# Shift and scale by output blocks, and R, K and V added up in six banks as inputs and weights arrive

## The chip, the cores and the metric

The kernel runs on one core of a Trainium2 chip. Its time is the device time of one execution in microseconds (us), the median of several. The first phase, which the change touches, is some 320 us of 3357. TensorE (PE) multiplies matrices, VectorE (DVE) and ScalarE (ACT) work on elements, GpSimd (POOL) and SyncE (SP) issue transfers here.

## What is computed

A trunk of two layers. Layer 0 mixes in time with RWKV-7, layer 1 with a pooling mixer; behind each comes a mixture of experts. The part that matters here is the beginning of layer 0, up to the scan:

```python
cond = jax.nn.silu(c)
mod = (cond @ ada_w[i] + ada_b[i]).reshape(B, N_MOD, D_MODEL)[:, :, None, :]
shift1, scale1, gate1, shift2, scale2, gate2 = (mod[:, n] for n in range(N_MOD))
h = x * (1 + scale1) + shift1
...
xx = jnp.pad(h, ((0, 0), (1, 0), (0, 0)))[:, :-1] - h
xs = h[None] + xx[None] * mu[:, None, None, :]
r, k, v = jnp.einsum('nbsd,nde->nbse', xs[:3], w_rkv)
w = -jax.nn.softplus(-(w0 + jnp.tanh(xs[3] @ w1) @ w2).astype(f32)) - 0.5
a = jax.nn.sigmoid(a0 + (xs[4] @ a1) @ a2)
g = jax.nn.sigmoid(xs[5] @ g1) @ g2
kk = (k * k_k).astype(f32).reshape(B, S, H, N)
kk = kk * lax.rsqrt(jnp.maximum(jnp.sum(kk * kk, axis=-1, keepdims=True), 1e-24))
```

There are 512 positions and 1024 columns (D), all float32. `w1` and `a1` have 64 columns, `g1` has 160. The modulation of both layers has 12 vectors of 1024: two of them (the shift and scale of `h`) are needed at once, ten later.

## The kernel before

The program is a row of phases with a barrier of all engines behind each. `phase_rwkv_products` is the first. D is cut in KT = 8 blocks of 128, the positions in TT = 4 tiles of 128; HALF is 512 columns.

**Modulation.** `cond` is one column for each block of 128 inputs. DVE multiplies a row block of `ada` (128 inputs x 1024 columns) by its column and adds it to an accumulator: eight such steps for one vector (lines 271 and 274 for the first two, 306 and 309 for the other ten, `add_mod`). PE then adds up the 128 partitions by products with a column of ones, eight for a vector (L352 for the first two, L361 in `sum_mod` for the others). SP loads the first two vectors' blocks into the buffers of `xs`, POOL the 80 blocks of the others into the four slots of `rw_g`, each when DVE is through with the block before it in that slot.

**Operands.** When both vectors are complete DVE makes `h` block by block (L287) and from it `xs[n]` in two instructions for each block: `shift_part` (L292) and `own_part` (L297). `xs` has two slots of 8 blocks, n goes to slot n % 2, and n >= 2 waits until the product that read the slot is through (`last_use`). The additions of `add_mod` stand in DVE's row behind the operands 1, 2 and 3 (`mods_after`: three vectors, three, four).

**Products.** PE makes one output of 128 x 512 after the other (`product`, L376) in a ring of four PSUM banks: eight matmuls that add up over the blocks of D, then ACT takes the bank (L432). R and K are made transposed, eight outputs of 128 columns each; V in four tiles of positions for each half of the columns. Each matmul of float32 leaves two rows in the trace. K's outputs are also squared (L442) and summed by head on PE (L383). The weights of R, K and V come in halves of 2 MB (SP, L228, L230 and L235) into two buffers, each when the products of the half before it in that buffer are done. `sum_mod` stands ahead of ten of the products (`sums_before`). Then follow the low-rank products: tanh (64 columns), decay `s` (65 rows with the bias), `ta` (64), the rate `aT` (eight outputs), `tg` (128 and 32 columns), the gate `g` (eight tiles of two matmuls).

**End.** PE turns the summed modulation columns (L420), DVE copies them (L344), SP stores them to `mod_rows` in HBM (L244). SP loads the constants of the scan into `held` (L242) when the last product that reads it is done, and waits for both. ACT's evacuations of the gate wait until the 80 additions are through, since they write `rw_g`. The next phase, the scan, begins on DVE at L632.

## Time and profile before

| | |
|---|---|
| median of 3 executions | 3357.09 us (3357.06 to 3357.4) |
| the profiled execution | 3357.63 us, span 3355.8 |
| mean granted clock of TensorE in it | 0.984 |
| PE busy | 3203.0 us, 95% of the span |
| DVE busy | 2593.2 us, 77% |
| first phase, up to the next one's first DVE instruction | 320.9 us |

Times of the trace count from the start of the span. A timeline names the start, the time from the first to the last instruction of a merged row, engine, line, output and inputs, shapes and count, and behind it in brackets how long the engine had been idle and what released it. The granted clock (PEclk) is 1.00 at 2.4 GHz and 0.5 at 1.2 GHz.

### The profile page before, as it was taken

What the parts mean: (1) busy time and instruction counts of PE and PEld (TensorE: products, weight loads), DVE (VectorE), ACT (ScalarE), POOL (GpSimd) and SP (SyncE); (2) the same over time, 40 slices, a digit from 0 to 9 for tenths busy, and PEclk for the clock granted to TensorE, in tenths of its full rate; (3) what the DMA queues carried; (4) which work ended last, traced back from release to release, by engine and by line L of the source; (5) the groups of instructions that cost most, each with busy time, mean ns of one, the idle gap of its engine ahead of it and who ended that gap; (6) DMA issues with size and microseconds to landing.
All of it is one profiled execution on the core that took longest, in us unless ns stands there. A gap on an engine that the chain in (4) does not pass through costs nothing. (4 is left out here: it accounts for less than half of the span.)

```text
span 3355.8 us, 56990 instructions
## 1 busy us (share of the span) xinstructions
PE 3203.0 (95%) x21428; PEld 2750.4 (82%) x21428; DVE 2593.2 (77%) x4747; ACT 1164.2 (35%) x1787; POOL 2053.4 (61%) x1303
## 2 busy tenths in 40 slices
PE   4998999799999999999999988999999999999998
PEld 2443888689999999888888866999999998888886
DVE  6672665479998888499888764899988866988997
ACT  0112455233324443333333432333344433333333
POOL 0211444267776555788888712677765558888884
PEclk9998999899999999999999989999999999999999
DMA  7870001267777887999999822687778979999995
GB/s 272 291 246 27 3 4 54 74 242 261 268 241 253 317 301 275 383 344 346 351 357 347 290 82 79 237 274 269 257 238 317 327 273 382 350 344 361 348 345 180
DMA packets 366859, 856.31 MB, mean 255 GB/s; under 512 B 32681, under 2 KB 201105, under 8 KB 358322
## 3 DMA queue, kind: packets, MB, share of 16 engines
q1 hardware_dynamic: 281394, 542.98, 46.8%
q0 software_dynamic: 85248, 310.42, 25.9%
q8 instruction: 139, 2.28, 0.3%
q14 instruction: 78, 0.64, 0.1%
HBM read 750.46 MB, written 102.81 MB: 254 GB/s over the span
## 5 line engine op out<-in xcount | busy, mean ns | idle before, releaser
L1683 PE MATMUL peer_acc<-peer_hhi,peer_uhi 128*128 128x384 f32 x2048 | 696.8, 340 | 8.9 <-POOL peer1same_ulo L1883 4.5
L1683 PE MATMUL peer_acc<-peer_hlo,peer_uhi 128*128 128x384 f32 x2048 | 685.8, 335 | 0.0
L1883 POOL TENSOR_TENSOR peer0same_ulo<-peer_u,peer_uhi 128x1024 fp32r<-128x1024 f32 x128 | 311.9, 2438 | 193.5 <-ACT peer_uhi L1763 192.8
L1883 POOL TENSOR_TENSOR peer1same_ulo<-peer_u,peer_uhi 128x1024 fp32r<-128x1024 f32 x128 | 312.0, 2439 | 191.8 <-ACT peer_uhi L1763 190.4
L1683 PEld LDWEIGHTS peer_acc<-peer_hhi,peer_uhi 128*128 128x128 f32 x2048 | 386.0, 188 | 12.5 <-POOL peer1same_ulo L1883 5.8
L1759 ACT ACTIVATE peer_gel<-peer_acc 128x384 f32<-128x384 f32 x256 | 125.9, 492 | 752.3 <-PE peer_acc L1683 677.6
L1683 PEld LDWEIGHTS peer_acc<-peer_hlo,peer_uhi 128*128 128x128 f32 x2048 | 385.9, 188 | 1.0 <-issue 0.5
L1914 POOL TENSOR_TENSOR peer0lsame_vlo<-peer0l_v,peer0l_vhi 128x1024 fp32r<-128x1024 f32 x128 | 310.8, 2428 | 85.2 <-ACT peer0l_vhi L1798 84.4
L1914 POOL TENSOR_TENSOR peer1lsame_vlo<-peer1l_v,peer1l_vhi 128x1024 fp32r<-128x1024 f32 x128 | 309.5, 2419 | 86.4 <-ACT peer1l_vhi L1798 85.3
L1946 DVE SCALAR_TENSOR_TENSOR peer_acc<-peer_row,peer_p_g,peer_acc 128x1024 f32<-128x1024 f32 x254 | 325.2, 1280 | 36.7 <-DMA peer_row<-in_pe_v,peer_idx 34.5
L1683 PE MATMUL peer_acc<-peer_hhi,peer0same_ulo 128*128 128x384 f32 x1024 | 343.6, 336 | 0.0
L1683 PE MATMUL peer_acc<-peer_hhi,peer1same_ulo 128*128 128x384 f32 x1024 | 343.4, 335 | 0.0
L1936 DVE SCALAR_TENSOR_TENSOR peer_row<-peer_row,peer_acc 128x1024 f32<-128x1024 f32 x256 | 308.4, 1206 | 0.1
L1722 PE MATMUL peer_acc<-peer0l_vhi,peer0l_phi 128*128 128x512 f32 x768 | 299.7, 390 | 3.7 <-DVE peer0l_plo L2044 2.3
L1722 PE MATMUL peer_acc<-peer1l_vhi,peer1l_phi 128*128 128x512 f32 x768 | 299.0, 389 | 2.8 <-DVE peer1l_plo L2044 1.5
L1722 PE MATMUL peer_acc<-peer0lsame_vlo,peer0l_phi 128*128 128x512 f32 x768 | 299.3, 390 | 0.0
L1722 PE MATMUL peer_acc<-peer0l_vhi,peer0l_plo 128*128 128x512 f32 x768 | 299.2, 390 | 0.0
L1722 PE MATMUL peer_acc<-peer1l_vhi,peer1l_plo 128*128 128x512 f32 x768 | 298.8, 389 | 0.0
L1722 PE MATMUL peer_acc<-peer1lsame_vlo,peer1l_phi 128*128 128x512 f32 x768 | 298.8, 389 | 0.0
L1864 POOL DMA_INDIRECT peer_row<-in_pe_v,peer_idx x256 | 271.5, 1061 | 42.5 <-issue 15.0
L1864 POOL DMA_INDIRECT peer_row<-in_pe_u,peer_idx x256 | 256.7, 1003 | 64.2 <-issue 38.9
L1763 ACT ACTIVATE peer_uhi<-peer_u 128x1024 fp32r<-128x1024 f32 x250 | 262.9, 1052 | 19.8 <-DMA peer_u<-in_pe_uT 19.8
(431 smaller groups left out, 6890.6 us busy)
## 6 DMA issues: line engine op xcount, KB each, us to landing
peer_u<-in_pe_uT SPq DMA_DIRECT2D x256, 512.0 KB
peer0l_v<-in_pe_v SPq DMA_DIRECT2D x128, 512.0 KB
peer1l_v<-in_pe_v SPq DMA_DIRECT2D x128, 512.0 KB
activations<-peer_gel SPq DMA_DIRECT2D x256, 192.0 KB
rw_g<-in_ada POOLq DMA_DIRECT2D x80, 512.0 KB
routing<-peer0m_wb SPq DMA_DIRECT2D x24, 1024.0 KB, 8.4
peer0l_wt<-routing SPq DMA_DIRECT2D x64, 384.0 KB
peer0l_gl<-activations SPq DMA_DIRECT2D x128, 192.0 KB
```

The lines of the kernel that those rows point to most:

```text
L1683: mm = pe.matmul(ub[e % 2][:, 0:SD], a, h[:, k, 0:SD], start=(n == 0), stop=(n == 3 * KT - 1))
L1722: mm = pe.matmul(acc[:, t, ds], a[:, ts], w[:, ds], start=(begin and n == 0), stop=(end and n == 2), skip_group_check=True)
L1759: a.activation(gel[:, e % NL], ub[e % 2][:, 0:SD], ACT.Gelu).then_inc(gel_made, 1)
L1763: a.activation(uhi[:, n % NH], u[:, n % NU], ACT.Copy).then_inc(uhi_made, 1)
L1864: g.indirect_dma_start(row[:, at % NG], None, table, bass.IndirectOffsetOnAxis(ap=idx[:, s:s + 1], axis=0)).then_inc(row_loaded[at % NG], 16)
L1883: g.tensor_tensor(ulo[:, q].rearrange("p k e -> p (k e)"), u[:, q].rearrange("p k e -> p (k e)"), uhi[:, e % NH].bitcast(F32).rearrange("p ...
L1914: g.tensor_tensor(vlo[:, q], vr[:, q], vhi[:, e % NH].bitcast(F32), ALU.subtract).then_inc(vlo_made, 1)
L1936: v.scalar_tensor_tensor(out=row[:, s % NG], in0=row[:, s % NG], scalar=1.0, in1=h_g, op0=ALU.mult, op1=ALU.mult, accum_out=dots[:, s:s + ...
L1946: v.scalar_tensor_tensor(out=acc_g, in0=row[:, s % NG], scalar=p_g[:, s:s + 1], in1=acc_g, op0=ALU.mult, op1=ALU.add).then_inc(acc_made, 1)
```

## The change

The host lays the first two modulation vectors out by blocks of output columns. A load now holds all 1024 inputs for 128 columns of one vector. For each block `k` of 128 columns:

- DVE adds up both vectors for these columns (`sum_first`, one tensor_scalar and seven scalar_tensor_tensor of 256 elements, each waiting for the one before). PE sums the partitions (two products with ones), DVE copies two columns and adds the bias, and makes `h` and `xs[0]` of this block. In DVE's row `sum_first(k + 1)` stands ahead of `make_h(k)`.
- PE takes the block as soon as it is there (`step`): six outputs in six PSUM banks get one matmul each. After eight steps the six are complete, and the two that are left are made as before (`rest`). K and V go the same way.
- The weights come in blocks of 128 rows x 1024 columns (0.5 MB) into twelve slots, eight of their own and four of `rw_s`. SP issues R's in turn with modulation and input blocks.

The ring has six banks instead of four. The first blocks' buffers are `rw_kT` and `rw_aT`. The tanh product stands behind V's steps and ahead of its two rests. `xs[5]` is made ahead of `xs[4]`, and the gate's first products ahead of the rate's. Four gate tiles stand ahead of the rate's eight outputs and four behind. The transpose of the modulation columns stands last. The ten vectors are added behind the operands 1, 2, 3 and 4 (two, four, two, two), and the reciprocal of the norm stands behind all of them.

```diff
-        w = arena("w", [P, 2, KT, HALF])
+        OWN, MORE = KT, TT
+        w_own = arena("w", [P, OWN, D])
+        w = [w_own[:, n] for n in range(OWN)] + [rw["s"][:, n] for n in range(MORE)]
...
+        NF = 4
+        first_w = [rw[n][:].rearrange("p k s -> p (k s)")[:, 2 * D * b:2 * D * b + 2 * D].rearrange("p (m k q) -> p m k q", m=2, q=P)
+                   for n in ("kT", "aT") for b in range(2)]
+        first_acc = [sq[:, b, 0:2 * P].rearrange("p (m q) -> p m q", q=P) for b in range(2)]
...
+        RING = 6
+        ps = ctx.enter_context(nc.psum_tensor("rwp_ps", [P, 8, 512], F32))
+        ring, mod_bank, norm_bank = [ps[:, b] for b in range(RING)], ps[:, 6], ps[:, 7]
...
+        TW = V0 + RING
+        V6 = TW + 1
+        S0 = V6 + KT - RING
+        TG = S0 + 2 * TT
+        TA = TG + 2
+        GA = TA + 1
+        A0 = GA + TT
+        GB = A0 + KT
+        END = GB + TT
+        xs_order = (0, 1, 2, 3, 5, 4)
+        slot_of = {0: 0, 1: 1, 2: 0, 3: 1, 5: 1, 4: 0}
+        free_after = {2: K0, 3: V0, 5: TW + 1, 4: S0}
+        mods_after = {1: 2, 2: 4, 3: 2, 4: 2}
         assert sum(mods_after.values()) == BESIDE_PRODUCTS
...
+            def load_first(k):
+                if k >= NF:
+                    sp.wait_ge(first_step, KT * (k - NF + 1))
+                for m in range(2):
+                    sp.dma_start(first_w[k % NF][:, m].rearrange("p k q -> p (k q)"), ada[m, k]).then_inc(first_loaded[k % NF], 16)
...
+            for k in range(KT):
+                if k + 1 < KT:
+                    load_first(k + 1)
+                sp.dma_start(hT[:, k, 1:S + 1], xT[:, k]).then_inc(x_loaded[k], 16)
+                load_w(0, k)
+            for k in range(MORE):
+                load_w(1, k)
...
+            sp.wait_ge(product_done, K0)
+            for k in range(MORE, KT):
+                load_w(1, k)
+            for k in range(KT - MORE):
+                load_w(2, k)
+            sp.wait_ge(product_done, V0)
+            for k in range(KT - MORE, KT):
+                load_w(2, k)
...
-            sp.wait_ge(product_done, G0)
+                sp.dma_start(dst, s).then_inc(low_loaded, 16)
+            sp.wait_ge(product_done, TA + 1)
             sp.dma_start(held[:, 0:scan_in.shape[1]], scan_in).then_inc(held_loaded, 16)
...
-            pool.wait_ge(first_used, NF)
+            pool.wait_ge(first_step, KT * 6)
...
+            def sum_first(k):
+
+                acc = first_acc[k % 2]
+                dve.wait_ge(first_loaded[k % NF], 32 * (k // NF + 1))
...
+                for i in range(KT):
+                    part = first_w[k % NF][:, :, i]
+                    if i == 0:
+                        v.tensor_scalar(acc, part, cond[:, 0:1], None, ALU.mult).then_inc(first_step, 1)
+                    else:
+                        dve.wait_ge(first_step, KT * k + i)
+                        v.scalar_tensor_tensor(out=acc, in0=part, scalar=cond[:, i:i + 1], in1=acc, op0=ALU.mult,
+                                               op1=ALU.add).then_inc(first_step, 1)
...
             def make_h(k):
+                dve.wait_ge(first_summed, k + 1)
+                v.tensor_copy(raw_of[:, :, k:k + 1], first_sums[k % 2][:, :, k:k + 1]).then_inc(raw_taken, 1)
+                dve.wait_ge(raw_taken, k + 1)
...
+            sum_first(0)
+            for k in range(KT):
+                if k + 1 < KT:
+                    sum_first(k + 1)
+                make_h(k)
+                shift_part(0, 0, k)
+                own_part(0, 0, k)
...
+
...
+            def step(n, k):
+
+                at, loaded = w_at(n, k)
+                pe.wait_ge(w_loaded[at], loaded)
+                pe.wait_ge(xs_made, KT * n + k + 1)
+                for m in range(RING):
+                    out = room(KT * n + m) if k == 0 else ring[(KT * n + m) % RING]
+                    mm = pe.matmul(out, *term(n, k, m), start=(k == 0), stop=(k == KT - 1), skip_group_check=True)
+                    if k == KT - 1:
+                        mm.then_inc(product_done, 1)
+                        count[0] += 1
+
+            def rest(n, m):
+                product(P, [term(n, k, m) for k in range(KT)])
...
+            pe.wait_ge(const_loaded, 16)
+            sum_first(0)
+            for k in range(KT):
+                if k + 1 < KT:
+                    sum_first(k + 1)
+                step(0, k)
+            rest(0, 6)
+            rest(0, 7)
+            sums_in = {(1, 3): 0, (1, 6): 1, (2, 1): 3, (2, 4): 4, (2, 6): 5}
+            for k in range(KT):
+                if (1, k) in sums_in:
+                    sum_mod(sums_in[1, k])
+                step(1, k)
+            pe.wait_ge(const_loaded, 32)
+            sum_squares(0)
+            sum_squares(1)
+            rest(1, 6)
+            sum_squares(2)
+            sum_squares(3)
+            sum_mod(2)
+            rest(1, 7)
+            sum_squares(4)
+            sum_squares(5)
+            for k in range(KT):
+                if (2, k) in sums_in:
+                    sum_mod(sums_in[2, k])
+                step(2, k)
+                if k == 0:
+                    sum_squares(6)
+                    sum_squares(7)
...
+            take(TW, tw[0:DL], ACT.Tanh, DL)
+            for j in range(RING, KT):
+                take_v(j)
...
             take(TA, ta[:], ACT.Copy, AL)
+            act.wait_ge(mod_used, BESIDE_PRODUCTS * KT)
+            take_gates(0)
             act.wait_ge(mod_summed, BESIDE_PRODUCTS)
             for m in range(KT):
...
+            take_gates(1)
...
+    first = made["ada"][:FIRST_MODS].reshape(FIRST_MODS, -1, P, x.shape[1] // P, P).transpose(0, 3, 2, 1, 4)
+    made["ada"] = np.concatenate([first.reshape(made["ada"][:FIRST_MODS].shape), made["ada"][FIRST_MODS:]])
```

TensorE at the start of the phase, before. `rwp_w` is here the accumulator of the modulation, then the weights:

```order
L352 MATMUL rwp_ps<-const_made,rwp_w 128x1 x16
L376 MATMUL rwp_ps<-rwp_xs,rwp_w 128x512 x40
L361 MATMUL rwp_ps<-const_made,rwp_mod_acc 128x1 x8
L376 MATMUL rwp_ps<-rwp_xs,rwp_w 128x512 x32
L361 MATMUL rwp_ps<-const_made,rw_aT 128x1 x8
```

And now:

```order
L398 MATMUL rwp_ps<-const_made,rwp_sq 128x1 x4
L430 MATMUL rwp_ps<-rwp_xs,rwp_w 128x512 x6
L398 MATMUL rwp_ps<-const_made,rwp_sq 128x1 x2
L430 MATMUL rwp_ps<-rwp_xs,rwp_w 128x512 x6
...
L398 MATMUL rwp_ps<-const_made,rwp_sq 128x1 x2
L430 MATMUL rwp_ps<-rwp_xs,rwp_w 128x512 x12
L411 MATMUL rwp_ps<-rwp_xs,rwp_w 128x512 x16
L430 MATMUL rwp_ps<-rwp_xs,rw_s 128x512 x18
L389 MATMUL rwp_ps<-const_made,rwp_mod_acc 128x1 x8
```

The 16 sums that stood ahead of all products now stand two by two ahead of the steps of R, and the first modulation sum of the ten has moved from R to K.

VectorE at the start of the phase, before (`rwp_xs` holds the loaded blocks of `ada`):

```order
L271 TENSOR_SCALAR rwp_w<-rwp_xs,const_cond 128x1024
L274 SCALAR_TENSOR_TENSOR rwp_w<-rwp_xs,const_cond,rwp_w 128x1024 x7
L271 TENSOR_SCALAR rwp_w<-rwp_xs,const_cond 128x1024
L274 SCALAR_TENSOR_TENSOR rwp_w<-rwp_xs,const_cond,rwp_w 128x1024 x7
L279 COPY const_mod_raw<-rwp_ps 128x16
```

And now (`rw_kT` and later `rw_aT` hold the loaded blocks, `rwp_sq` the accumulator):

```order
L301 TENSOR_SCALAR rwp_sq<-rw_kT,const_cond 128x256
L304 SCALAR_TENSOR_TENSOR rwp_sq<-rw_kT,const_cond,rwp_sq 128x256 x7
L309 COPY const_mod_raw<-rwp_ps 128x2
L311 TENSOR_TENSOR const_modT<-const_mod_raw,rwp_bias_73 128x2
L314 TENSOR_SCALAR rwp_hT<-rwp_hT,const_modT 128x512
L319 TENSOR_SCALAR rwp_xs<-rwp_hT,const_cols 128x512
L324 SCALAR_TENSOR_TENSOR rwp_xs<-rwp_hT,rwp_mu_70,rwp_xs 128x512
```

The 16 long instructions have become 64 short ones, and one block of `h` and `xs[0]` follows each eight of them instead of all following the sixteenth.

TensorE behind V, before:

```order
L361 MATMUL rwp_ps<-const_made,rwp_mod_acc 128x1 x8
L376 MATMUL rwp_ps<-rwp_xs,rw_held 64x512 x8
L376 MATMUL rwp_ps<-rwp_w,rwp_tw 128x512 x8
L361 MATMUL rwp_ps<-const_made,rw_aT 128x1 x8
L376 MATMUL rwp_ps<-rwp_xs,rw_held 64x512 x8
L376 MATMUL rwp_ps<-rwp_ta,rwp_w 128x512 x8
L376 MATMUL rwp_ps<-rwp_xs,rw_held 128x512 x8
L376 MATMUL rwp_ps<-rwp_xs,rw_held 32x512 x8
L420 MATMUL rwp_ps<-const_made,const_mod_raw 96x128
L376 MATMUL rwp_ps<-rwp_w,rwp_tg 128x512 x16
```

And now, from behind the last product of V:

```order
L411 MATMUL rwp_ps<-rwp_w,rwp_tw 128x512 x8
L389 MATMUL rwp_ps<-const_made,rw_aT 128x1 x8
L411 MATMUL rwp_ps<-rwp_xs,rw_held 128x512 x8
L411 MATMUL rwp_ps<-rwp_xs,rw_held 32x512 x8
L411 MATMUL rwp_ps<-rwp_xs,rw_held 64x512 x8
L389 MATMUL rwp_ps<-const_made,rwp_mod_acc 128x1 x8
L411 MATMUL rwp_ps<-rwp_w,rwp_tg 128x512 x8
L389 MATMUL rwp_ps<-const_made,rw_aT 128x1 x8
L411 MATMUL rwp_ps<-rwp_ta,rwp_w 128x512 x8
L411 MATMUL rwp_ps<-rwp_w,rwp_tg 128x512 x8
L509 MATMUL rwp_ps<-const_made,const_mod_raw 96x128
```

The tanh product has gone ahead of V's last two, the gate's first products (128 and 32 columns) ahead of the rate's (64), three of the ten modulation sums stand here where two stood, and the transpose is last.

## Rows read from the trace of the kernel before

**Rows 1.** The page: busy time of TensorE.
```profile
PE 3203.0 (95%) x21428; PEld 2750.4 (82%) x21428; DVE 2593.2 (77%) x4747; ACT 1164.2 (35%) x1787; POOL 2053.4 (61%) x1303
```

**Rows 2.** Stretches: length, busy of PE, PEld, DVE, ACT, POOL; clock; DMA; GB/s.
```profile
0.00:48.60 48.60, 6.96 (x32) 6.90 (x32) 23.84 (x30) 1.49 (x2) 2.54 (x8) 1.00 0.86 326
48.60:109.00 60.40, 59.73 (x145) 26.80 (x146) 46.70 (x58) 4.18 (x7) 12.18 (x23) 1.00 0.78 266
109.00:241.30 132.30, 132.30 (x393) 62.02 (x392) 84.52 (x88) 14.79 (x25) 28.23 (x53) 1.00 0.80 271
241.30:279.70 38.40, 33.88 (x74) 14.31 (x73) 22.86 (x41) 9.84 (x13) 0.00 (x0) 0.73 0.00 0
```

**Rows 3.** Timeline of VectorE, 6 to 49 us.
```profile
6.48 9.25 DVE L274 SCALAR_TENSOR_TENSOR rwp_w<-rwp_xs,const_cond,rwp_w 128x1024 f32<-128x1024 f32 x7 [0.45 <-DMA rwp_xs<-in_ada]
...
45.16 0.17 DVE L280 TENSOR_TENSOR const_modT<-const_mod_raw,const_cols 128x16 f32<-128x16 f32 x1
...
46.89 0.54 DVE L287 TENSOR_SCALAR rwp_hT<-rwp_hT,const_modT 128x512 f32<-128x512 f32 x1
47.35 0.48 DVE L292 TENSOR_SCALAR rwp_xs<-rwp_hT,const_cols 128x512 f32<-128x512 f32 x1
47.75 0.74 DVE L297 SCALAR_TENSOR_TENSOR rwp_xs<-rwp_hT,rwp_mu,rwp_xs 128x512 f32<-128x512 f32 x1
```

**Rows 4.** Timeline of TensorE: the start of R.
```profile
48.63 5.72 PE L376 MATMUL rwp_ps<-rwp_xs,rwp_w 128*128 128x512 f32 x8 [3.79 <-DVE rwp_xs L297]
...
56.12 30.51 PE L376 MATMUL rwp_ps<-rwp_xs,rwp_w 128*128 128x512 f32 x70 [0.39 <-DVE rwp_xs L297]
```

**Rows 5.** Timeline of ScalarE: evacuations in R, its last one, V's last one.
```profile
66.06 0.60 ACT L432 ACTIVATE rw_rT<-rwp_ps 128x512 f32<-128x512 f32 x1 [6.27 <-PE rwp_ps L376]
...
95.32 0.60 ACT L432 ACTIVATE rw_rT<-rwp_ps 128x512 f32<-128x512 f32 x1 [8.06 <-PE rwp_ps L376]
...
109.05 0.60 ACT L432 ACTIVATE rw_rT<-rwp_ps 128x512 f32<-128x512 f32 x1 [6.27 <-PE rwp_ps L376]
...
240.70 0.60 ACT L432 ACTIVATE rw_v<-rwp_ps 128x512 f32<-128x512 f32 x1 [6.27 <-PE rwp_ps L376]
```

**Rows 6.** Timeline of TensorE: decay, a modulation sum, rate, gate.
```profile
253.87 13.73 PE L376 MATMUL rwp_ps<-rwp_w,rwp_tw 65*128 65x512 f32 x16 [4.52 <-ACT rwp_tw L432]
267.39 3.41 PE L361 MATMUL rwp_ps<-const_made,rw_aT 128*128 128x1 f32 x16
...
280.41 7.13 PE L376 MATMUL rwp_ps<-rwp_ta,rwp_w 64*128 64x512 f32 x16 [0.68 <-ACT rwp_ta L432]
...
302.27 16.92 PE L376 MATMUL rwp_ps<-rwp_w,rwp_tg 128*128 128x512 f32 x32 [0.43 <-ACT rwp_tg L432]
```

**Rows 7.** Stretches of the low-rank products, columns as in rows 2.
```profile
254.00:258.00 4.00, 4.00 (x5) 1.49 (x6) 3.96 (x7) 2.11 (x3) 0.00 (x0) 0.52 0.00 0
...
274.00:276.00 2.00, 2.00 (x5) 0.64 (x4) 0.00 (x0) 0.00 (x0) 0.00 (x0) 0.84 0.00 0
...
280.00:288.00 8.00, 7.59 (x17) 3.21 (x18) 0.00 (x0) 5.59 (x9) 0.00 (x0) 1.00 0.00 1
```

**Rows 8.** Timeline of VectorE: two groups of eight additions.
```profile
183.62 0.74 DVE L306 TENSOR_SCALAR rwp_mod_acc<-rw_g,const_cond 128x1024 f32<-128x1024 f32 x1
...
195.89 0.75 DVE L306 TENSOR_SCALAR rw_aT<-rw_g,const_cond 128x1024 f32<-128x1024 f32 x1
...
208.28 1.28 DVE L309 SCALAR_TENSOR_TENSOR rw_aT<-rw_g,const_cond,rw_aT 128x1024 f32<-128x1024 f32 x1 [0.79 <-DMA rw_g<-in_ada]
```

**Rows 9.** Timeline at the phase's end, and DMA issues with us to landing.
```profile
319.23 0.60 ACT L432 ACTIVATE rw_g<-rwp_ps 128x512 f32<-128x512 f32 x1 [1.51 <-PE rwp_ps L376]
320.90 0.17 DVE L632 TENSOR_SCALAR scan_omka<-const_cols 128x8 f32<-128x8 f32 x1 [18.32 <-PEq L78]
...
const_cols<-in_cols SPq DMA_DIRECT2D x1, 96.0 KB, 2.0
mod_rows<-rwp_sq SPq DMA_DIRECT2D x1, 48.0 KB, 4.8
```

More of the change, by code:

```diff
@@ L431, in take, with take_v, take_gates @@
                 act.wait_ge(product_done, n + 1)
[L432 removed]
+                nc.scalar.activation(out, ring[n % RING][0:width, :], func, bias=bias).then_inc(evacuated, 1)
+            def take_v(j):
+                half, t = divmod(j, TT)
+                n = V0 + j if j < RING else V6 + j - RING
+                take(n, rw["v"][:, t, half * HALF:(half + 1) * HALF], ACT.Copy)
+            def take_gates(half):
+                for t in range(TT):
+                    take((GA, GB)[half] + t, rw["g"][:, t, half * HALF:(half + 1) * HALF], ACT.Copy)
             act.wait_ge(cols_loaded, 16)
```

225 lines of the change are left out of this document (91 added, 134 removed).

## Prediction

> **What bounds the kernel now.** I read the page's shares first, then the stretches, then the timelines of TensorE (PE), VectorE (DVE) and ScalarE (ACT), and last the moment at which the next phase starts. The share of 95% for PE [rows 1] hides a first phase in which PE is not the limit everywhere. A barrier ends each phase, so whatever the first phase saves is saved at the end of the kernel too. The stretches [rows 2] cut that phase up. Up to 48.6 us PE works 6.96 us: it waits while DVE adds up the shift and scale products of all 1024 columns. Up to 109 it forms R, up to 241.3 K and V, without a gap. Up to 279.7 it stands idle for 4.5 us behind the tanh of the decay product and then runs at 0.73 of its clock. Then come the rest of the low-rank products. The next phase's first DVE instruction starts at 320.90 [rows 9]. The change touches this phase only, so I work out when that instruction starts in the changed kernel.
>
> **Prices on PE.** One product of eight matmuls takes ACT's idle time plus its instruction, 6.27 + 0.60 = 6.87 us [rows 5], or 0.859 us a matmul. A product with a sum of modulation columns in front took 8.06 + 0.60 = 8.66 us [rows 5], so such a sum costs 1.79 us. From the last R evacuation (109.05) to the last V one (240.70) are 131.65 us [rows 5]: 16 products, 7 such sums, 8 sums of squares. Single matmuls that each have another bank cost no more: 7.13 us for eight (the row of 280.41) [rows 6].
>
> **R, by steps.** This is the largest term. Now R starts at 48.63 [rows 4] and its last evacuation starts at 109.05. Afterwards DVE makes the first 128 columns of shift and scale, one input block and one block of R's operand, and PE runs six matmuls on it while DVE works on the next block.
> DVE's chained instruction now: seven of 1024 elements end after 9.25 us [rows 3], (9.25 - 1.28)/6 = 1.33 us from start to start, so 0.05 over its duration. The same operation took 0.74 us for 512 elements [rows 3] and 1.28 for 1024; on that line 256 elements take 0.47, chained 0.52. The first of each eight is a tensor_scalar, 0.48 for 512 [rows 3] and 0.74 for 1024 [rows 8], so 0.35, chained 0.40. A block costs 0.40 + 7 x 0.52 = 4.04 us. The row of 512 elements is the upper bound: 0.79 chained, or 1.9 us more a block. The lower one, with the fixed part alone (0.17 us) [rows 3], is not near; the line decides.
> The Trainium skill ("VectorE: DVE Perf Modes", section on the TRN2 errata) says that each instruction pays a fixed cost and that tiles should have at least 512 elements, which speaks against 256. Its formula for tensor_tensor gives an estimated 0.42 us for 256 elements, and with it a block would cost some 0.3 us less, so its advice is right in sign and small in size here.
> Behind the block come copy and add, 0.21 each from start to start (0.17 and a gap of 0.04) [rows 3], the shift-and-scale of the input (0.54 + 0.05) [rows 3], the shifted part (0.48 + 0.05) and the own part (0.74): 2.23 us, 2.28 with rounding up of the gaps. The period is 6.3 us. The first megabyte can't be there before 6.5 us, since the second half megabyte landed at 6.48 [rows 3]. DVE ends R's operand at 6.5 + 8 x 4.04 + 8 x 2.28 = 57 us. The gain is that PE has then done seven of its eight steps.
> PE's step is 6 x 0.859 = 5.15 us and four small records, about 0.5: less than the period. The first step runs in part at 1.2 GHz: the first eight records took 5.72 us where the higher level has 8 x 0.436 = 3.5 (70 records in 30.51 us) [rows 4]. I take 2 us, which the shorter step makes up for. Bounds: nothing, and 5.15 us for each step at the lower level. Last step: PE is through step six at 54.7 + 5.2 = 59.9, so the eighth ends at 65 and the two left-over products at 65 + 13.7 = 79 us. That is 30 us before 109.05, and the 1.79 us sum that stood in R is now in K.
> Transfers. By 57 us these loads must be in: 16 of 0.52 MB for the modulation, 8 of 0.26 for the input, 8 of 0.52 for R's weights, 0.3 MB else: 15.0 MB. At the 326 GB/s of the first stretch [rows 2] that is 46 us. They are hidden, if SP's queue isn't stopped: from the fifth block on a load waits for a buffer that DVE frees three blocks earlier, some 20 us before the data is needed. If that cover went, each us late would be a us lost.
>
> **K and V.** The matmuls are the same in number; PE waits for DVE at no step, since the operand of K is ready at 57 + 8.5 = 66. One tanh product (6.87) moves in between. Seven modulation sums stand in this stretch as before. 79 + 131.65 + 6.87 = 217.5 us. DVE in between: two groups of eight additions cost 12.3 + 13.7 = 26.0 us (183.62 to 195.89, and to 208.28 + 1.28) [rows 8]. By this pace the fourth operand is ready at about 175, where PE wants it at 194, and each sum finds its additions done.
>
> **After V.** Gone is the idle time: the tanh is taken while PE does two V products (4.5 us). The eight decay products took 13.73 us at a granted clock of 0.52 [rows 6, 7]; with the clock still up they cost 7.13, as the eight of 280.41. So does the sum of 3.41 us [rows 6]: 1.79. What then stands in PE's row: decay 7.13, sum 1.79, two gate products 13.74, rate product 6.87, sum 1.79, four gate tiles 8.46 (half of 16.92) [rows 6], sum 1.79, rate 7.13, four tiles 8.46: 57.2 us. PE ends at 217.5 + 57.2 = 274.7. Late next is DVE's last pair of groups: the sixth operand waits for V's end, 217.5 + 8.5 = 226, plus 26.0 = 252; PE wants it before its last sum, at 257.7. Six us of cover; the 1.1 MB for the next phase, issued at about 247, can eat up to 4 of them.
>
> **The tail.** New on the path is the transpose of the modulation columns, now behind all products. It releases a DVE copy of one small block (0.3 at most by the 0.17) [rows 3] and a store. The store took 4.8 us to land [rows 9] behind 1.1 MB that SP had issued a us before; the 96 KB load at the start took 2.0 us. I take 2.0, as nothing is in its way, and keep 4.8. With 0.4 for the transpose and 0.5 of waiting (estimates, from hand-overs of 0.04 to 0.45) [rows 3, 4]: 3.2, and from the end of the phase's last work to the next phase 320.90 - 319.83 = 1.07 us [rows 9]. The next phase starts at 274.7 + 4.3 = 279.0.
>
> **Sum.** 320.9 - 279.0 = 41.9 us. The profiled execution took 3357.63 us, 0.54 above the median of 3357.09. 3357.09 - 41.9 = 3315.2 us, ratio 1.0126.
>
> **Rivals.**
> A. The clock falls in narrow products. For: the decay products with 65 rows ran at 0.52 for their whole length, and the level rose only in 274 to 276, in 128-row work [rows 7]. Against: the 64-row ones of 280 to 288 kept 1.00 [rows 7]. If it falls after the last sum, 7.13 + 8.46 us double: 3331; if behind the decay products, some 7 us: 3322.
> B. The clock swings between its levels in R's steps, since PE waits 0.6 us in each. If half of each step is at 1.2 GHz a step takes 5.15 + 2.6 + 0.5 = 8.2 us, over DVE's 6.3, and R ends 15 us later: 3330. The Trainium skill ("TensorE: Matmul & The Clock Gate", section "A second HAM failure mode: psum-queue depth-cycling") says that a kernel which cycles through PSUM banks idles briefly between groups often enough for this. Against, in this trace: the wait of 0.39 us ahead of 56.12 left 0.436 us a record behind it [rows 4].
> C. Slower: the same in all 24 steps of R, K and V, at the lower level throughout. Each costs 5.15 us more: 24 x 5.15 = 124, so 3439. It decides from the ninth step on (41.9/5.15 = 8.1). Against: K's and V's steps have no waits.
> D. The weights come too late, and the steps don't overlap, so the change doesn't do what it says: R then ends at 57 + 55 = 112 instead of 79: 3348.
> E. The last additions are late, by the slower pace of loads and the next phase's 1.1 MB: 4 to 8 us, 3321.
>
> **How the numbers follow.** Forecast 3315.2 +- 5: 0.55. A: 0.14, B: 0.08, C: 0.02, D: 0.04, E: 0.12. Below 3310 (a DVE chain nearer to its lower bound): 0.05. The range takes in A, E and most of B: 3308 to 3333. A measurement here tells 0.2% (6.7 us) from no change. Faster by more: all but C and half of D, 0.94. Within 0.2%: 0.03. Slower: 0.03.
>
> **What would show it.** PE's first 512-column record at 17 us, R's last evacuation near 79 (above 85 speaks for B, above 100 for D), the last V evacuation near 217, a granted clock of 1.00 from 25 us to 274, no wait of PE for the modulation additions near 257, the next phase's first DVE instruction at 279. Wrong is the sum if one DVE instruction on 256 elements takes over 0.6 us from start to start, or if PE ends before 270.

## The result, and the profile after

| kernel | median us (runs, from to) | ratio to before, 95% interval |
|---|---|---|
| before | 3357.24 (4, 3357.06 to 3357.58) | |
| after | 3326.49 (4, 3324.36 to 3328.18) | 0.9908 [0.9891, 0.9925] |

The change saves 30.8 us, where 41.9 were forecast. The profiled execution took 3326.24 us for a span of 3324.3. On the chips of the experiments the kernel before took between 3350 and 3360 us, so some us of its time move from run to run; the ratios carry that.

The page of after. PE's busy time is 3 us above before [rows 1], although it does the same products:

```profile
PE 3206.4 (96%) x21428; PEld 2750.0 (83%) x21428; DVE 2601.7 (78%) x4810; ACT 1161.7 (35%) x1786; POOL 2054.3 (62%) x1303
```

**The start.** VectorE's timeline, in the columns of [rows 3]: the seven chained additions of a block on 256 elements, and the end of R's operand, all eight blocks of it, at 55.3.

```profile
7.03 3.61 DVE L304 SCALAR_TENSOR_TENSOR rwp_sq<-rw_kT,const_cond,rwp_sq 128x256 f32<-128x256 f32 x7
...
54.55 0.75 DVE L324 SCALAR_TENSOR_TENSOR rwp_xs<-rwp_hT,rwp_mu,rwp_xs 128x512 f32<-128x512 f32 x1
```

Before, only the first block was ready at 48.5 [rows 3]. The last two of the eight were made by this instruction pair of before:

```profile
56.38 1.41 DVE L297 SCALAR_TENSOR_TENSOR rwp_xs<-rwp_hT,rwp_mu,rwp_xs 128x512 f32<-128x512 f32 x2
```

So the whole operand stood at 57.8 before and stands 2.5 us earlier now. The gain in R does not come from there but from what PE has done by then.

TensorE's timeline, in the columns of [rows 4]: the first step of R and the two products left over.

```profile
16.86 7.81 PE L430 MATMUL rwp_ps<-rwp_xs,rwp_w 128*128 128x512 f32 x12 [1.25 <-DVE rwp_xs L324]
...
63.67 13.90 PE L411 MATMUL rwp_ps<-rwp_xs,rwp_w 128*128 128x512 f32 x32
```

ScalarE's timeline: the last evacuations of R and of V, which answer to 109.05 and 240.70 in [rows 5].

```profile
77.60 0.60 ACT L515 ACTIVATE rw_rT<-rwp_ps 128x512 f32<-128x512 f32 x1 [6.27 <-PE rwp_ps L411]
...
215.25 0.60 ACT L515 ACTIVATE rw_v<-rwp_ps 128x512 f32<-128x512 f32 x1 [8.05 <-PE rwp_ps L411]
```

R's last evacuation stands 31.5 us earlier than before and V's last one 25.5: the tanh product between them has moved ahead of V's end.

**Behind V.** TensorE's timeline of the low-rank products, which answers to [rows 6]. In this order: decay, a sum of modulations, the products with the gate's and the rate's first weights (48 records, three products), a sum, four gate tiles, the last sum, rate, four gate tiles, the transposition.

```profile
215.05 7.03 PE L411 MATMUL rwp_ps<-rwp_w,rwp_tw 65*128 65x512 f32 x16
221.92 2.31 PE L389 MATMUL rwp_ps<-const_made,rw_aT 128*128 128x1 f32 x16
224.09 24.02 PE L411 MATMUL rwp_ps<-rwp_xs,rw_held 128*128 128x512 f32 x48
248.04 1.95 PE L389 MATMUL rwp_ps<-const_made,rwp_mod_acc 128*128 128x1 f32 x16
249.84 8.48 PE L411 MATMUL rwp_ps<-rwp_w,rwp_tg 128*128 128x512 f32 x16
258.25 1.95 PE L389 MATMUL rwp_ps<-const_made,rw_aT 128*128 128x1 f32 x16
260.13 13.51 PE L411 MATMUL rwp_ps<-rwp_ta,rwp_w 64*128 64x512 f32 x16
273.56 16.09 PE L411 MATMUL rwp_ps<-rwp_w,rwp_tg 128*128 128x512 f32 x16
289.59 0.45 PE L509 MATMUL rwp_ps<-const_made,const_mod_raw 128*96 128x128 f32 x1
```

No row has a wait in brackets: PE is busy all the time. But rate takes 13.51 us and the last four gate tiles 16.09, where the first four take 8.48. The stretches, in the columns of [rows 2] (the clock is the third number from the end), say why:

```profile
222.00:224.00 2.00, 2.00 (x17) 2.00 (x15) 2.00 (x5) 1.13 (x3) 0.00 (x0) 0.78 0.03 8
224.00:226.00 2.00, 2.00 (x5) 0.97 (x5) 1.79 (x3) 0.00 (x0) 0.53 (x1) 0.50 0.00 0
...
230.00:232.00 2.00, 2.00 (x6) 0.95 (x5) 0.93 (x2) 0.00 (x0) 0.53 (x1) 1.00 1.01 371
...
250.00:258.00 8.00, 8.00 (x16) 2.18 (x16) 2.46 (x1) 1.79 (x3) 0.00 (x0) 1.00 0.29 122
...
260.00:262.00 2.00, 2.00 (x5) 1.04 (x5) 1.22 (x6) 0.00 (x0) 0.00 (x0) 0.67 0.00 0
...
282.00:290.00 8.00, 8.00 (x9) 1.73 (x8) 0.00 (x0) 1.18 (x3) 0.00 (x0) 0.50 0.00 0
```

The granted clock falls to 0.50 (1.2 GHz) twice: for some 7 us from within the first sum on (223 to 230), and at about 261 us, from where it stays down to the end of the phase. Both times PE had no idle time ahead of it.

**The tail.** The phase's end, in the columns of [rows 9]. The store took 1.5 us to land, where [rows 9] have 4.8:

```profile
290.14 0.29 DVE L379 COPY rwp_sq<-rwp_ps 96x128 f32<-96x128 f32 x1 [28.45 <-PE rwp_ps L509]
...
293.29 0.17 DVE L724 TENSOR_SCALAR scan_omka<-const_cols 128x8 f32<-128x8 f32 x1 [2.86 <-PEq L78]
...
mod_rows<-rwp_sq SPq DMA_DIRECT2D x1, 48.0 KB, 1.5
```

The next phase starts 27.6 us earlier, and the profiled execution is 31.4 us shorter. Part of the rest came in a later phase that the change doesn't touch. A stretch of 50 us, which starts equally far behind the next phase's start (within 0.2 us), in before (first fence) and in after:

```profile
1367.80:1417.80 50.00, 46.98 (x251) 44.49 (x251) 18.14 (x16) 16.43 (x23) 37.24 (x23) 0.97 1.04 408
```

```profile
1340.30:1390.30 50.00, 48.52 (x264) 45.66 (x263) 21.59 (x19) 17.80 (x25) 37.95 (x24) 1.00 1.03 402
```

The mean granted clock was 0.97 there before and 1.00 after. These two executions can't say whether that is of the change or of the run.

### The profile page after: what moved, and what is told of

Read it like the earlier page. It is cut to its first block and busy times, and to the rows that moved or that the text cites. A ratio compares the mean times of both kernels' runs of the same rounds, so it can differ in the third digit from the quotient of the medians.

```text
span 3324.3 us, 57085 instructions
## 1 busy us (share of the span) xinstructions
PE 3206.4 (96%) x21428; PEld 2750.0 (83%) x21428; DVE 2601.7 (78%) x4810; ACT 1161.7 (35%) x1786; POOL 2054.3 (62%) x1303
```

## The experiments

All kernels are the changed one with one edit; zero_turn has two. The main question is what brings the clock down behind V and costs 14 us; the others are what the steps of R, and those of K and V, are worth. "Next phase" is the start of the next phase's first DVE instruction in the profiled execution, 293.29 in after.

| kernel | median us (runs, from to) | ratio to before, 95% interval | next phase |
|---|---|---|---|
| sum9_early | 3340.72 (4, 3338.53 to 3341.55) | 0.9948 [0.9931, 0.9964] | 306.33 |
| dense_between | 3334.25 (4, 3320.13 to 3336.69) | 0.9932 [0.9916, 0.9949] | 284.47 |
| rate_first | 3339.13 (4, 3338.5 to 3340.66) | 0.9945 [0.9929, 0.9962] | 303.17 |
| r_after_all | 3365.14 (7, 3361.78 to 3369.15) | 1.0026 [1.0015, 1.0037] | 329.19 |
| short_sums | 3322.09 (5, 3305.95 to 3326.33) | 0.9900 [0.9883, 0.9916] | 270.96 |
| wide_rows | 3308.35 (4, 3307.75 to 3314.07) | 0.9864 [0.9848, 0.9881] | 272.31 |
| spread_sums | 3322.16 (4, 3314.84 to 3333.43) | 0.9911 [0.9883, 0.9938] | 277.04 |
| turn_early | 3327.78 (4, 3325.95 to 3328.23) | 0.9915 [0.9899, 0.9932] | 291.30 |
| zero_rows | 3309.15 (4, 3307.34 to 3311.2) | 0.9856 [0.9840, 0.9873] | 272.59 |
| zero_turn | 3306.98 (4, 3305.45 to 3307.82) | 0.9852 [0.9835, 0.9868] | 271.05 |
| kv_whole | 3363.9 (10, 3361.51 to 3369.25) | 1.0021 [1.0011, 1.0031] | 333.10 |
| gate_rows | 3314.7 (4, 3310.41 to 3319.17) | 0.9875 [0.9859, 0.9892] | 280.64 |

### Other orders of the low-rank products

**sum9_early**: the last sum ahead of the first four gate tiles.

```diff
             sum_mod(8)
+            sum_mod(9)
             gates(0)
-            sum_mod(9)
             pe.wait_ge(evacuated, TA + 1)
```

> In the changed kernel (3326.5 us) the granted clock of TensorE falls to 0.50 at about 260 us, at the end of the last modulation sum, and the eight rate products (13.51 us) and the last four gate tiles (16.09) run at half speed: 14 us over my sum. Edit: the last sum of one-column products stands ahead of the first four gate tiles instead of between them and the rate products. Theory N (a long run of narrow products without 128-row work lets the clock fall): still eight gate tiles and eight rate products in one run, so it falls again, 3324 to 3328 us. Rival S (the 1.9 us of one-column products just ahead of the rate products do it): the clock stays at 1.00, 3312.5 us.

**dense_between**: the rate's first product, on 128 rows, between the first gate tiles and the last sum. Here and in rate_first the numbering of the products and ScalarE's evacuations follow the new order.

```diff
-            pe.wait_ge(xs_made, 6 * KT)
-            product(AL, [(a1[:, k], xs[:, slot_of[4], k]) for k in range(KT)])
...
             gates(0)
+            pe.wait_ge(xs_made, 6 * KT)
+            product(AL, [(a1[:, k], xs[:, slot_of[4], k]) for k in range(KT)])
             sum_mod(9)
```

> Edit: the product of the rate's first factor (128 rows, 7 us) stands between the first four gate tiles and the last modulation sum instead of ahead of them. Theory N: the run of narrow products is broken, the clock stays at 1.00, 3312 to 3314 us. Rival S: the last sum still stands just ahead of the rate products, so the clock falls there, about 3326 us.

**rate_first**: both last sums, rate, and then all eight gate tiles.

```diff
-            gates(0)
             sum_mod(9)
...
                 product(P, [(a2[:, m * P:(m + 1) * P], ta[:])])
+            gates(0)
             gates(1)
```

> Edit: both last modulation sums and then the eight rate products stand ahead of all eight gate tiles. Theory N: the narrow run is as long as before (sums 3.7, rate 7.1, gate 16.9 us), the clock falls somewhere in the gate tiles or rate products, 3318 to 3328 us. Rival S: two sums in a row stand just ahead of the rate products, so it falls at once and both rate and gate double, up to 3335 us. If the rate products with 64 rows are what matters and not the gate's, 3312 us.

All three are slower than after by their medians (dense_between's interval still meets after's). TensorE's timeline of sum9_early:

```profile
245.01 1.95 PE L389 MATMUL rwp_ps<-const_made,rwp_mod_acc 128*128 128x1 f32 x16
253.21 3.57 PE L389 MATMUL rwp_ps<-const_made,rw_aT 128*128 128x1 f32 x16 [6.26 <-DVE rw_aT L336]
256.65 16.08 PE L411 MATMUL rwp_ps<-rwp_w,rwp_tg 128*128 128x512 f32 x16
272.65 14.02 PE L411 MATMUL rwp_ps<-rwp_ta,rwp_w 64*128 64x512 f32 x16
```

PE waits 6.26 us for VectorE's last additions, the clock falls in that wait, and nothing behind it brings it back: rate and gate are narrow (64 rows; 128 and 32 rows), and they run at 0.50 for over 45 us. rate_first has a wait of 3.05 us in the same place and the same end. So neither kernel could tell the two theories apart. dense_between has no such wait, only one of 0.67 us. The clock of its profiled execution fell in the first gate tiles:

```profile
238.15 1.95 PE L389 MATMUL rwp_ps<-const_made,rwp_mod_acc 128*128 128x1 f32 x16 [0.67 <-ACT rwp_tg L515]
239.96 14.48 PE L411 MATMUL rwp_ps<-rwp_w,rwp_tg 128*128 128x512 f32 x16
254.37 9.24 PE L411 MATMUL rwp_ps<-rwp_xs,rw_held 128*64 128x512 f32 x16
263.54 1.95 PE L389 MATMUL rwp_ps<-const_made,rw_aT 128*128 128x1 f32 x16
265.41 7.13 PE L411 MATMUL rwp_ps<-rwp_ta,rwp_w 64*128 64x512 f32 x16
272.47 8.50 PE L411 MATMUL rwp_ps<-rwp_w,rwp_tg 128*128 128x512 f32 x16
```

The product on 128 rows took 9.24 us, between its 7.1 at the full clock and twice that: the clock came back in it. From there the narrow products ran at 1.00 to the end of the phase. That is also the pattern of before, where [rows 7] show the clock rising in 128-row work and the 64-row product of [rows 6] at 7.13 behind it. But the three other executions took 3334 to 3337 us, so the order doesn't hold the clock. Two suspects were left: the sums, 2 us of products with one column each, which stood right ahead of or at the head of each fall that had no long wait, and the narrow rows of what follows.

### Sums or rows

**short_sums**: sums 7, 8 and 9 as one product of eight columns each.

```diff
             def sum_mod(n):
                 pe.wait_ge(mod_used, KT * (n + 1))
+                if n >= 7:
+                    mm = pe.matmul(mod_bank[:, n * KT:(n + 1) * KT], mod_sum[n % 2][:, 0:P], ones[:, 0:KT], ...)
```

> The last three sums of modulations (numbers 7, 8 and 9) are one product with eight columns each in place of eight products with one column; their values are not the reference's, all else is as in the changed kernel. Every fall of the clock seen so far began in such a sum or right behind it (after: 260 us, behind the sum at 258.25; the kernel whose decay gate is made up ahead of the last gates: 242, behind the sum at 238.15). Theory P (the stretch of one-column products is what brings the clock down): it stays at 1.00 to the end of the phase; the sums save 3 x 1.6 = 5 us, the rate product takes 7.1 instead of 13.5 and the last gate tiles 8.5 instead of 16.1, the short loss in the product behind sum 7 (24.0 against 21.1) goes as well: 3326.5 - 5 - 14 - 3 = 3304 us. Theory W (products on 64 or 128+32 rows, wherever they stand in the tail, bring it down): the clock falls at about the same place, and only the sums' 5 us go: 3321.5.

**wide_rows**: other operands of 128 rows in the narrow products.

```diff
-    product(P, [(tg[:, 0, t * P:(t + 1) * P], g2a[:, cs]), (tg[0:GR, 1, t * P:(t + 1) * P], g2b[:, cs])])
+    product(P, [(tg[:, 0, t * P:(t + 1) * P], g2a[:, cs]), (tg[:, 0, t * P:(t + 1) * P], g2a[:, cs])])
...
-    product(P, [(a2[:, m * P:(m + 1) * P], ta[:])])
+    product(P, [(g2a[:, m * P:(m + 1) * P], tg[:, 0])])
```

> The rate product and the second half of each gate product take 128 rows of other operands already there, in place of 64 and of 32 rows; as many products with as many columns, so at a full clock the same time; the values of rate and gate are not the reference's. Theory W (too few rows bring the clock down): it stays at 1.00 behind 260 us, rate product 7.1, last gate tiles 8.5: 3326.5 - 14 = 3312.5 us. Theory P (the one-column products of the sums do it, whatever follows): it falls at about 260 as before, and comes back once full products have run: the rate product at 0.50 for some of its length, then 1.00; between 3313 and 3326, and 0.50 seen at 262.

**spread_sums**: all sums, but between other products.

```diff
-            sum_mod(7)
...
-            product(P, [(g1[:, k, 0:P], xs[:, slot_of[5], k]) for k in range(KT)])
+            product(P, [(g1[:, k, 0:P], xs[:, slot_of[5], k]) for k in range(KT)], between=7)
...
-            product(AL, [(a1[:, k], xs[:, slot_of[4], k]) for k in range(KT)])
+            product(AL, [(a1[:, k], xs[:, slot_of[4], k]) for k in range(KT)], between=8)
```

> The same sums, all computed, but each one-column product stands between two products of the gate's and the rate's first weights (sums 7 and 8) or, four at a time, ahead of the last two of the first four gate tiles (sum 9). No work is saved. Theory P: no stretch of 2 us of one-column products is left, the clock stays at 1.00: 3326.5 - 14 - 3 = 3309.5 us. Theory W: it falls as before in the narrow products: 3326.5. A third way: it falls at the first four gate tiles, since the stretch behind it is less dense, 8 us more: 3334.

wide_rows gave 3308.35 us, 4 better than theory W said, in all four executions below any of after. The operands and with them the row count were changed there, and the three sums stood as in after. Its TensorE timeline, the three products behind the first sum and then from the last sum on:

```profile
223.47 21.11 PE L411 MATMUL rwp_ps<-rwp_xs,rw_held 128*128 128x512 f32 x48
...
253.26 1.84 PE L389 MATMUL rwp_ps<-const_made,rw_aT 128*128 128x1 f32 x16
254.97 7.11 PE L411 MATMUL rwp_ps<-rwp_tg,rwp_w 128*128 128x512 f32 x16
261.92 7.03 PE L411 MATMUL rwp_ps<-rwp_w,rwp_tg 128*128 128x512 f32 x16
```

The part that theory W left out: the gate tiles take 7.1 us for four, not 8.48. Two gains of 1.4 us each come with the full rows themselves. A third difference has nothing to do with the rows: the three products behind the first sum took 21.11 us, where after has 24.02. The decay products ahead of them had 65 rows here as in after, and yet the clock stayed up. Of the profiled executions that leave this place as it is in after, those of rate_first, sum9_early, wide_rows, gate_rows and kv_whole have 21.11 us here (dense_between, with two of the three products, has 14.10), those of turn_early and r_after_all a fall (22.80 and 24.03). So the first, short fall comes in some executions and not in others.

short_sums is split. The profiled execution took 3305.95 us, and its clock stayed at 1.00 to the end of the last gate tiles, through 8.47, 7.13 and 8.50 us of narrow products: theory P's number. The four others took 3321.1 to 3326.3, at a mean granted clock of 0.979 to 0.981 against its 0.987: theory W's number. spread_sums gave 3315.24 (profiled, at 1.00 through the whole tail) and 3314.84, then 3329.07 and 3333.43, the last two at 0.979. The long executions have no trace, so where their clock fell isn't shown; by times and mean clocks the narrow products can lose the clock without the blocks of one-column products too. That these blocks are not enough for a fall is shown by the traces: with full rows behind them the clock stayed up. That they aren't needed rests on the times alone.

### A version that computes everything

**zero_rows**: what the narrow products lack in rows is filled with zeros in one operand; the other holds whatever weights lie there.

```diff
-        tw, ta, tg = arena("tw", [DL + 1, S]), arena("ta", [AL, S]), arena("tg", [P, 2, S])
+        tw, ta, tg = arena("tw", [P, S]), arena("ta", [P, S]), arena("tg", [P, 2, S])
...
+            ch.send(v.memset(tg[:, 1], 0.0))
+            ch.send(v.memset(ta[AL:P], 0.0))
+            ch(v.memset(tw[DL:P, :], 0.0))
             v.memset(tw[DL:DL + 1, :], 1.0).then_inc(row_made, 1)
...
-    product(P, [(tw[:, t * P:(t + 1) * P], w2[:, half * HALF:(half + 1) * HALF])])
+    product(P, [(tw[:, t * P:(t + 1) * P], w[0][:, half * HALF:(half + 1) * HALF])])
...
-    product(P, [(a2[:, m * P:(m + 1) * P], ta[:])])
+    product(P, [(w[1][:, m * P:(m + 1) * P], ta[:])])
...
-    product(P, [(tg[:, 0, t * P:(t + 1) * P], g2a[:, cs]), (tg[0:GR, 1, t * P:(t + 1) * P], g2b[:, cs])])
+    product(P, [(tg[:, 0, t * P:(t + 1) * P], g2a[:, cs]), (tg[:, 1, t * P:(t + 1) * P], w[3][:, cs])])
```

> The decay, rate and gate products run on 128 rows: the rows that the operands lack (63 of decay, 64 of rate, 96 of each gate tile's second product) are zero in the moved or held operand made by the kernel and hold whatever weights lie there in the other. Everything is computed, with the same number of products and columns. Theory W1 (it is the rows that pass through the array which the clock follows, whatever their values): as in the kernel with other operands in these rows, the clock stays at 1.00 to the end of the last gate tiles and the time is about 3308 us. Theory W2 (it is the work on values that are not zero): the rows of zeros change nothing and it falls at about 260 us as in the changed kernel: 3326.5. The three clearings by DVE stand ahead of its first work, which waits for a load until 6.6 us; at 0.3 to 0.7 us each they are done before it.

**gate_rows**: the same for the gate tiles alone.

```diff
+            ch(v.memset(tg[:, 1], 0.0))
...
-    product(P, [(tg[:, 0, t * P:(t + 1) * P], g2a[:, cs]), (tg[0:GR, 1, t * P:(t + 1) * P], g2b[:, cs])])
+    product(P, [(tg[:, 0, t * P:(t + 1) * P], g2a[:, cs]), (tg[:, 1, t * P:(t + 1) * P], w[3][:, cs])])
```

> The rows of zeros of the kernel with full rows, in the gate tiles' second products alone; decay stays on 65 rows and rate on 64. The gate tiles should be as short as there (7.1 us for four instead of 8.5: the second products run beside nothing shorter), 2.8 us less in all. If the 32-row products of the gate tiles are what brings the clock down, it stays at 1.00 and the time is about 3309 us, as with all rows full; if 8 products on 64 rows in a row behind the last sum suffice to bring it down, it falls in the rate product (at about 257 us) and stays there or comes back in the last gate tiles: 3316 us if it comes back, 3323.5 if it doesn't.

zero_rows took 3309.15 us, as wide_rows did (3308.35), so it doesn't matter that the added rows multiply zeros. Its TensorE timeline:

```profile
215.18 7.03 PE L414 MATMUL rwp_ps<-rwp_w,rwp_tw 128*128 128x512 f32 x16
...
246.59 7.11 PE L414 MATMUL rwp_ps<-rwp_w,rwp_tg 128*128 128x512 f32 x16
253.54 1.84 PE L392 MATMUL rwp_ps<-const_made,rw_aT 128*128 128x1 f32 x16
255.25 7.11 PE L414 MATMUL rwp_ps<-rwp_ta,rwp_w 128*128 128x512 f32 x16
262.20 7.03 PE L414 MATMUL rwp_ps<-rwp_w,rwp_tg 128*128 128x512 f32 x16
```

These 128 rows cost what 65 cost (7.03 us for 16 records). The next phase starts 20.7 us earlier than in after, and the time is 17.3 us shorter. Some 3.4 of the 20.7 us are the short fall behind the decay products, which this execution doesn't have; as six executions with 65 rows there don't have it either, it can't be credited to the zeros. gate_rows lies between. Two rows of its TensorE timeline, and its stretches from the rate product on:

```profile
254.64 13.17 PE L412 MATMUL rwp_ps<-rwp_ta,rwp_w 64*128 64x512 f32 x16
267.74 9.53 PE L412 MATMUL rwp_ps<-rwp_w,rwp_tg 128*128 128x512 f32 x16
```

```profile
255.00:272.00 17.00, 17.00 (x21) 6.31 (x20) 1.03 (x6) 5.94 (x9) 0.00 (x0) 0.52 0.01 1
274.00:277.00 3.00, 3.00 (x8) 1.27 (x7) 0.00 (x0) 1.07 (x2) 0.00 (x0) 1.00 0.00 0
```

The clock falls in the 64-row product, the only narrow work since the decay products 33 us earlier, though a sum of one-column products stands right ahead of it. In the gate tiles with filled rows it comes back, which it never did in the unfilled ones of after. The forecast of 3316 for this case fits the profiled execution (3316.78, mean clock 0.983). The other three took 3310 to 3319 at 0.984 to 0.985; the longest of them has 0.985, so its time isn't explained by this fall.

### The transposition

**turn_early**, and **zero_turn**, which is zero_rows with the same edit:

```diff
-            gates(1)
-            assert count[0] == END
             pe.wait_ge(raw_made, 1)
             pe.transpose(mod_bank[0:modT.shape[1], 0:P], raw[:], const["ident"][:]).then_inc(raw_turned, 1)
+            gates(1)
+            assert count[0] == END
```

> The transposition of the modulations and with it their copy and store stand ahead of the last four gate tiles instead of behind them. The tail behind the last product (0.4 + 0.3 + 0.3 + 1.5 + 1.1 us) is then beside the gate tiles; what is left is the last evacuation of 0.6 us and the phase's end of about 1 us. The next phase starts 2.5 to 3.5 us sooner: 3323.5 us. Should PE wait for the modulations' additions by DVE ahead of the transposition (they end at about 262, in the rate product), the gain would be the same, since it has 11 us to spare.

> As the kernel with rows of zeros, and with the transposition ahead of the last four gate tiles. By theory W1 3308 less the 2 us by which the next phase began sooner with the transposition alone: 3306; by theory W2 3325.

The next phase starts 2.0 us earlier in the first and 1.5 in the second. The times don't tell that: turn_early lies 1.3 us above after, zero_turn 2.2 below zero_rows, both within their intervals. zero_turn is the shortest version that computes everything, some 50 us (1.5%) under before; that it beats zero_rows isn't shown.

### What the steps are worth

**r_after_all**: PE starts the steps of R when the whole operand is made.

```diff
             for k in range(KT):
                 if k + 1 < KT:
                     sum_first(k + 1)
+            pe.wait_ge(xs_made, KT)
+            for k in range(KT):
                 step(0, k)
```

> Edit: TensorE takes its sums of the first modulation as before but starts R's steps only when the whole operand of R is there (55.3 us in the changed kernel's trace). Theory O (the gain is that R's matmuls run beside VectorE's chain): R ends at 55.3 + 2.4 + 55 = 113 us instead of 78, so 35 us are lost: 3361 us. Rival L (the gain comes from the earlier and finer loads and from the other order behind V): 3326 to 3340 us.

**kv_whole**: K and V as whole products, R by steps.

```diff
+            def whole(n, m):
+                for k in range(KT if m == 0 else 0):
+                    at, loaded = w_at(n, k)
+                    pe.wait_ge(w_loaded[at], loaded)
+                    pe.wait_ge(xs_made, KT * n + k + 1)
+                rest(n, m)
...
-            for k in range(KT):
-                if (1, k) in sums_in:
-                    sum_mod(sums_in[1, k])
-                step(1, k)
+            for m in range(RING):
+                if (1, m + 1) in sums_in:
+                    sum_mod(sums_in[1, m + 1])
+                whole(1, m)
```

> K and V are made as whole products, one tile after the other; R alone is made in steps. The forecast counted nothing for the stepping of K and V (131.65 us for the two, as before). But four of the eight blocks of weights of each are asked for only when the product ahead has ended (at 77.6 us for K, first landing some 4 us later), and a whole product needs all eight. Theory A (the steps of K and V bring nothing): same as the changed kernel, 3326.5. Theory B (they cover the late blocks): PE waits for the last block at the head of K and again at the head of V, some 5 us each, while V7's rest or the like can't stand in: 3326.5 + 10 = 3336, with two waits of PE on the DMA of weights in the profile.

r_after_all took 3365.14 us. ScalarE's last evacuation of R stands at 113.52, 35.9 us later than in after, and the next phase starts 35.9 us later too. So the overlap of R with VectorE's work is worth 39 us in time, more than the whole gain; without it the change is slower than before. One reason is the start of R: 55.54 us, where before could begin at 48.63 [rows 4] with the first block of the operand; R's last evacuation is 4.5 us later than before. Rivals C and D of the prediction are out by after's own rows: its steps overlap, and those behind the first run at the full clock (10.54 us for 24 records in the last two).

kv_whole surprised: 37 us slower, not 10. TensorE's timeline at the first product of K and of V:

```profile
92.00 5.87 PE L411 MATMUL rwp_ps<-rwp_xs,rw_s 128*128 128x512 f32 x8 [14.99 <-DMA rwp_w<-in_rw_w_rkv]
...
176.54 6.26 PE L411 MATMUL rwp_ps<-rwp_w,rwp_xs 128*128 128x512 f32 x8 [15.96 <-DMA rw_s<-in_rw_w_rkv]
```

The mechanism is theory B's, three times its size. SP issues K's late blocks from 77.04 us on, eight blocks of weights within 5 us, and PE can start only 15 us later. The DMA engines are full meanwhile: they moved 5.8 MB in those 15 us, 388 GB/s, and 3.2 MB of them are the modulation weights of GpSimd's queue. How long the loads would take alone wasn't tried. PE comes back from each wait at the lower clock (5.87 and 6.26 us for eight records, where 3.6 is the full clock's time). Up to the end of V the two waits cost 35.5 us (decay begins at 250.51, in after at 215.05). In after the same blocks are as late (14.9 us from issue to landing, the median of the eight), but K's steps don't need them at once. Two rows of after's TensorE timeline, the first three steps of K and the seventh and eighth:

```profile
77.40 15.61 PE L430 MATMUL rwp_ps<-rwp_xs,rw_s 128*128 128x512 f32 x36
...
111.79 10.55 PE L430 MATMUL rwp_ps<-rwp_xs,rwp_w 128*128 128x512 f32 x24
```

The fifth step is the first that needs a late block and begins at 99.79, some 22 us behind K's beginning; the eighth begins some 40 us behind it. So the steps hide a delay that the change's own loading order makes: before had whole products of K and V and no such wait. The forecast's zero for the steps of K and V was right in its sum, but it named nothing that they hide.

## Why the prediction was right, and where its sum was off

The range of 3308 to 3333 held the time and the sign was right. The forecast was 11.3 us too low, in the main by one term.

- **R.** The chained instruction of 256 elements took 3.61/7, 0.52 us, as put. The first block's weights came at 6.6 (6.5 forecast), the period was 6.07 us (6.3), the operand was ready at 55.3 (57), the last evacuation came at 77.60 (79). The first step cost 2.4 us at the lower clock (7.81 us against 5.40 for the later ones), where 2 were taken. By 55.3 PE had done six steps and was in the seventh, as the sum has it; the sentence that says seven is one too many. Rival B didn't happen, but its condition wasn't met either: behind its late first step PE was busy up to 53 us and waited 0.30 us once. Whether short waits in each step would bring the clock down isn't shown.
- **K and V.** 137.65 us from the last R to the last V evacuation; 131.65 + 6.87 = 138.5 forecast.
- **After V.** 57.2 us were forecast, and from 215.05 to the transposition at 289.59 it was 74.5. Of these 17 us, 6.4 stand in rate (13.51 against 7.13), 7.6 in the last gate tiles (16.09 against 8.46), 3.4 in the three products behind the first sum (24.02 against 20.6). This is the step that failed, and it is rival A, given 0.14: the narrow products were priced from the rows of 280.41 and 302.27 [rows 6], which ran at 1.00. Ahead of the rate there, 128-row work had just raised the clock [rows 7]; with the new order four gate tiles and a sum stand there instead. The argument against rival A, that the 64-row products of [rows 7] kept 1.00, took this as a property of the product, and the runs show that the same 64-row products run at either level. That the order decides is not shown: in its trace dense_between ran the rate at 7.13 us with 128-row work ahead of it again, but by their times and clocks its three other executions did worse (3334 to 3337 us, 0.978 to 0.979 against 0.984). What the runs do show is that with rate and gate on 128 rows it stays up (wide_rows, zero_rows, zero_turn). The other terms came as put: decay 7.03 (7.13), the first gate tiles 8.48 (8.46). The first part of rival A (the fall behind the last sum: 3331) has the place right; it gave 4.5 us too much: it counted 15.6 us for what took 14.0, and the start, the tail and the later phases were better than the sum.
- **The last additions** were done at 249.2, ahead of the last sum at 258.25: rival E didn't happen. sum9_early shows what a wait there costs: with its 6.26 us the next phase starts 13 us later, since the clock went down in it and the first gate tiles took 16.08 us instead of 8.48.
- **The tail** was 3.7 us from the transposition to the next phase, 4.3 forecast. The terms add up: the products behind V began 2.4 us earlier than put (215.05, not 217.5), and -2.4 + 17.3 - 0.6 is 14.3; the next phase started at 293.29 instead of 279.0.
- **Behind the phase.** The forecast said that what the first phase saves is saved at the end. It was 27.6 us at the next phase and 31.4 at the end, or 30.8 by the medians. So the later phases, which are the same in both kernels, can give 4 us or take them (zero_rows lost 5 of its 20.7 us there, by the profiled executions). Spells at the lower clock, as in the stretches above, are a part of that; how much of it isn't shown.
- **The chances.** By the forecast's own rule, all but C and half of D, the chance of "faster by more" is 0.96 and not 0.94.

The Trainium skill ("TensorE: Matmul & The Clock Gate", section "HAM oscillation — how this bites in real kernels") has as its rule that PE may have no long idle gaps. The waits of sum9_early and kv_whole agree with it. After doesn't: its clock fell at 261 us with PE busy from 215 to 290 without a gap, so idle time is not the only cause, and the measurement decides.

What stays open: when exactly a narrow stretch brings the clock down. By times and mean clocks the same kernel (short_sums, spread_sums, dense_between) did and didn't lose the clock, or lost it for shorter, in different executions, and only one execution of each has a trace.

## What to carry to other kernels

A product's price at the full clock holds only with the work that stood ahead of it: before moving it, read the granted clock there and the rows of its neighbours, not only its own duration. Where products with fewer than 128 rows stand in a row, try them filled up with rows of zeros: that cost no time on PE here and gave 17 us. And a product made in steps by input blocks is worth what it lets begin early or come late: 39 us for R's operand, 37 us for the weights of K and V, which this loading order brings late, though the matmuls are the same.

## What the runs showed of the hardware that was not expected

- The granted clock went to 0.50 under a PE that was busy throughout, in products on 64 rows (13.17 us for 16 records in gate_rows, 7.13 at 1.00) and in or behind one-column products. With rate and gate on 128 rows it stayed at 1.00 in all three traces (wide_rows, zero_rows, zero_turn), and rows of zeros counted as much as rows of data (3309.15 against 3308.35 us).
- Once down, it stayed down through 30 us of busy narrow products (after, 260 to 290) and came back in full-row ones: the product of 9.24 us in dense_between, the filled gate tiles of 9.53 us in gate_rows.
- Four gate tiles took 8.48 us with a second product on 32 rows and 7.11 with it on 128: the shorter contraction was the slower one.
- The same narrow products ran at either level: at 0.50 in after, and at 1.00 through 24 us of them in the traced execution of short_sums (3305.95 us). Its four others took 3321 to 3326 us, as if the clock had fallen.
- A wait of PE can cost twice: behind the 6.26 us in sum9_early the next phase started 13 us later. Part of that can come without a wait: in kv_whole the clock fell in the same gate tiles (14.07 us) with PE busy.
